# Half steps per head for layer 1's attention, gates ahead of branch products in `at`, and split folds

## The reference, cut to what matters

```python
for l in range(DEPTH):
    sh1, sc1, gt1, sh2, sc2, gt2 = adaln(c, w_ada[l], b_ada[l])     # silu(c) @ w_ada: [1024] x [1024, 6144]
    hx = modulate(rms_norm(x, g_mix[l]), sh1, sc1)
    px = split_cols(hx @ w_in[l], IN_SIZES)     # q, k, v, conv, short conv, fourier, 4 gates
    y_attn = windowed_latent_attention(q, k, v, kc, vc, sink)
    x = x + gt1 * mixer_output(px, y_attn, ...)
    x = x + gt2 * conv_ffn(modulate(rms_norm(x, g_ffn[l]), sh2, sc2), ...)

def mixer_output(p, y_attn, ...):
    y_conf, y_sc, y_fn = local_branches(...)    # y_conf = silu(layer_norm(dwconv31(a * sigmoid(g))))
    gates = split(sigmoid(p_gate), 4)
    m = gates[0] * (y_attn @ w_br[0])
    for g, y, w in zip(gates[1:], (y_conf, y_sc, y_fn), w_br[1:]):
        m = m + g * (y @ w)
    return m @ w_out
```

## Time and profile before

| | us |
|---|---|
| median of 3 runs | 1331.49 |
| lowest, highest | 1329.52, 1332.81 |
| the profiled execution's own time | 1331.0 |
| its span on the core | 1329.2 |
| around the span | 1.8 |

### The profile page before, as it was taken

One profiled execution on the slowest core, in us unless ns is written; L12 is line 12 of the kernel. 1 busy time (PEld: TensorE's weight loads), 2 busy tenths in 40 slices (PEclk: granted clock), 3 DMA queues, 4 the chain that ended last, 5 costly groups with the idle time before them and its releaser, 6 DMA issues.

```text
span 1329.2 us, 19887 instructions
## 1 busy us (share of the span) xinstructions
PE 1268.8 (95%) x7661; PEld 1096.8 (83%) x7661; DVE 884.4 (67%) x1203; ACT 555.7 (42%) x872; POOL 290.9 (22%) x247
## 2 busy tenths in 40 slices
PE   5999999999999999999999999999999998999997
PEld 3788877777788788787788888889878898999997
DVE  4694488653699568995756664576676566765654
ACT  4322345643343244331233332244566455653543
POOL 0003499111223001111001120003772130120210
PEclk9999999999999999999999999999999999999999
DMA  9463222213456315664555664235333454564560
GB/s 377 154 210 115 77 75 65 68 64 94 137 178 235 104 46 178 204 206 160 188 165 189 189 213 146 94 106 173 119 110 110 145 175 143 177 216 146 188 207 33
DMA packets 50339, 198.76 MB, mean 150 GB/s; under 512 B 5584, under 2 KB 6992, under 8 KB 49104
## 3 DMA queue, kind: packets, MB, share of 16 engines
q1 hardware_dynamic: 50256, 197.62, 45.3%
HBM read 196.55 MB, written 1.05 MB: 149 GB/s over the span
## 4 chain that ended last, share of the span: by engine, by line
PE 74%; DVE 17%; issue 5%; ACT 4%; DMA 0%; DVEq 0%; SPq 0%; ACTq 0%
PE psA L490 21%; PE psA L491 21%; PE psA L492 21%; DVE ada_sum L1228 4%; DVE w_lo L1207 4%; DVE acc L1443 2%; PE psB L490 2%; PE psB L492 2%; PE psB L491 2%; ACT w_hi L914 1%; DVE small L1456 1%; PE psB L759 1%; PE psB L747 1%; PE psB L663 1%; PE psA L732 1%
## 5 line engine op out<-in xcount | busy, mean ns | idle before, releaser
L490 PE MATMUL psA<-h_hi,w_hi 128*128 128x256 f32 (+1 forms) x1544 | 525.5, 340 | 9.0 <-DVE h_lo L1321 4.9
L491 PE MATMUL psA<-h_lo,w_hi 128*128 128x256 f32 (+1 forms) x1544 | 517.9, 335 | 0.0
L492 PE MATMUL psA<-h_hi,w_lo 128*128 128x256 f32 (+1 forms) x1544 | 517.8, 335 | 0.0
L914 ACT ACTIVATE w_hi<-raw 128x1024 fp32r<-128x1024 f32 (+2 forms) x244 | 277.0, 1138 | 341.5 <-PE psA L492 233.9
L1207 DVE TENSOR_TENSOR w_lo<-raw,w_hi 128x1024 fp32r<-128x1024 f32 (+2 forms) x244 | 332.8, 1364 | 127.8 <-ACT w_hi L914 127.1
L490 PEld LDWEIGHTS psA<-h_hi,w_hi 128*128 128x128 f32 x1544 | 296.4, 192 | 42.5 <-issue 7.6
L492 PEld LDWEIGHTS psA<-h_hi,w_lo 128*128 128x128 f32 x1544 | 296.3, 192 | 29.1
L491 PEld LDWEIGHTS psA<-h_lo,w_hi 128*128 128x128 f32 x1544 | 296.7, 192 | 28.1 <-issue 0.5
L479 POOL TENSOR_TENSOR hid_lo<-sig,hid_hi 128x512 f32 (+3 forms) x44 | 68.4, 1555 | 484.2 <-ACT hid_hi L1171 484.2
L1228 DVE SCALAR_TENSOR_TENSOR ada_sum<-raw,csil,ada_sum 128x1024 f32<-128x1024 f32 x112 | 158.2, 1443 | 0.0
L490 PE MATMUL psA<-hid_hi,w_hi 128*128 128x256 f32 (+1 forms) x352 | 118.4, 336 | 3.7 <-DVE sig L1634 2.1
(11 more groups left out here) (189 smaller groups left out, 1440.5 us busy)
## 6 DMA issues: line engine op xcount, KB each, us to landing
raw<-w_up SPq DMA_DIRECT2D x88, 512.0 KB, 4.2
raw<-w_ada SPq DMA_DIRECT2D x80, 512.0 KB, 3.5
raw<-w_dn SPq DMA_DIRECT2D x32, 704.0 KB, 5.0
raw<-w_in SPq DMA_DIRECT2D x36, 512.0 KB, 3.8
raw<-w_at SPq DMA_DIRECT2D x24, 512.0 KB, 3.5
raw<-w_fn SPq DMA_DIRECT2D x16, 640.0 KB, 3.9
raw<-w_sc SPq DMA_DIRECT2D x16, 640.0 KB, 3.9
raw<-w_cf SPq DMA_DIRECT2D x16, 640.0 KB, 4.0
```

Source lines behind the costliest of these rows:

```text
L490: pe.matmul(out, w0, hi, start=first, stop=False)
L491: pe.matmul(out, w0, lo, start=False, stop=False)
L492: return pe.matmul(out, w1, hi, start=False, stop=last)
L914: act.activation(w_hi[:, s, 0:tiles * P], raw[:, r, 0:tiles * P], ACT.Copy).then_inc(head_done, 1)
```

## The change

- In layer 1 a unit's two heads are weighed, turned and copied in two places rather than one: head 0 at place 2k (exp) and 2k+2 (turn), head 1 at 2k+1 and 2k+3; `values` comes at 2k+4. `share` stands at the start of ScalarE's place 2k+2, `weight_sum` behind the multiplication of the odd place.
- Layer 1 has two branch banks (`mix_bank`: psB[1], psB[3]) and turns both heads through psB[0]. Gates wait for the tanh two steps before, no longer for the multiplication.
- `at` follows the order `AT_ORDER`: (group, part), part 2 being the branch product. Gates stand one to two steps ahead of the branch products that they belong to; the layer norm's reciprocal moves from step 8 to 7, its silu from 9 to 8, its last rest from 10 to 9.
- The modulation groups 3 and 4 begin two steps later; the second of the two folds of a group moves one step on, and so does `REDUCE` for groups 3 to 7.
- SyncE's reload of `x` waits for the end of `at` as well, since `q` now holds gates.

```diff
-ADA_START = {2: START["in"] + 2, 3: START["at"] + 3, 4: START["at"] + 11}
+ADA_START = {2: START["in"] + 2, 3: START["at"] + 5, 4: START["at"] + 13}
...
-REDUCE = {START["out"] + 3 if _g == 4 else ADA_START[_g] + 10: _g for _g in ADA_START}
+REDUCE = {START["out"] + 4 if _g == 4 else ADA_START[_g] + 10 + (3 <= _g < 8): _g for _g in ADA_START}
+ADA_END = {ADA_START[_g] + 8: _g for _g in ADA_START}
+AT_ORDER = [(0, 0), (0, 1), (1, 0), (1, 1), (0, 2), (2, 0), (2, 1), (1, 2), (3, 0), (3, 1), (2, 2), (3, 2)]
...
+        def mix_bank(layer, n):
+            return psB[1] if layer and n % 2 else psB[3]
+        def turn_bank(layer, half):
+            return psB[0 if layer else half]
...
+        def halves_at(layer, place, late):
+            if layer == 0:
+                return [(place - late, half) for half in range(2)] if 0 <= place - late < NB[0] else []
+            k, half = divmod(place - late, 2)
+            return [(k, half)] if 0 <= k < NB[1] else []
+        LATE = [{"turn": 1, "value": 2}, {"turn": 2, "value": 4}]
...
                 for idx in range(LEN["sc"]):
-                    pe.wait_ge(evac, st.n - 1)
-                    merge(st, y_hi[:, 2:4, :], y_lo[:, 2:4, :], 2, 8 + idx, mix_bank,
-                          [(sc_rest, 2 * layer + 2), (evac, st.n)])
+                    pe.wait_ge(sigd, 34 * layer + 2 + 8 + idx - 1)
+                    merge(st, y_hi[:, 2:4, :], y_lo[:, 2:4, :], 2, 8 + idx, mix_bank(layer, st.n),
+                          [(sc_rest, 2 * layer + 2), (evac, st.n - layer)])
...
+                def turn(k, half):
+                    pe.wait_ge(pn, 2 * (b0 + k) + half + 1)
+                    if layer:
+                        pe.wait_ge(pt, 2 * (b0 + k) + half)
...
                         else:
-                            pe.wait_ge(evac, m0 + 3 * (group - 1))
+                            pe.wait_ge(sigd, 34 * layer + 18 + 2 * (group - 2) + part + 1)
...
                 def attend(place):
+                    k = at_place(layer, place, LATE[layer]["value"])
+                    if k is not None:
+                        attended(k)
+                    for k, half in halves_at(layer, place, LATE[layer]["turn"]):
+                        turned(k, half)
+                    for k, half in halves_at(layer, place, 0):
+                        weigh(k, half)
                 def attend_late(place):
+                    k = at_place(layer, place, LATE[layer]["turn"])
+                    if k is not None:
                         share(k)
...
+            def ada_fold(g, vv):
+                op = dve.tensor_reduce(ada_part[:, vv, :], ada_sum[:, vv, :].rearrange("p (b k) -> p b k", k=32),
+                                       AX.X, ALU.add, apply_transpose=True)
+                if vv == ada_vectors(8 * g) - 1:
                     op.then_inc(folded, 1)
...
+                    if st.n in ADA_END and ada_vectors(8 * ADA_END[st.n]) == 2:
+                        ada_fold(ADA_END[st.n], 1)
...
                         dve.scalar_tensor_tensor(t, sg, 1.0, ps, ALU.add, ALU.mult).then_inc(evac, 1)
+                        if place is not None and layer and place % 2:
+                            weight_sum(place // 2)
```

More of the change, by code:

```diff
@@ L326, in program, with at_place @@
         B0 = [0, NB[0]]
-        def step_at(layer, place):
-            k = place if layer == 0 else (place + 1) // 2 if place % 2 == 0 or place == 17 else None
-            return k
+        def at_place(layer, place, late):
+            count, every = NB[layer], 1 + layer
+            k, odd = divmod(place - late, every)
+            return k if odd == 0 and 0 <= k < count else None
+        def halves_at(layer, place, late):
[4 more added lines that the diff above has]
+        LATE = [{"turn": 1, "value": 2}, {"turn": 2, "value": 4}]
+        PLACES = [18, 19]
         def wide(layer, k):
@@ L462, in _ @@
                     add(n0 + START["sc"], idx, idx, gtmp[idx % 2])
-                for idx in range(2, LEN["at"], 3):
+                for group in range(4):
                     for half in range(2):
-                        add(n0 + START["at"], idx, idx // 3 * 2 + half, (gtmp if idx == 2 else tmp)[half])
+                        add(n0 + START["at"], 3 * group + 2, 2 * group + half, (gtmp if group == 0 else tmp)[half])
                 for idx in range(LEN["cf"]):
@@ L804, in _ @@
                     st = Step(m0 + idx, idx)
-                    group, part = divmod(idx, 3)
+                    group, part = AT_ORDER[idx]
                     pe.wait_ge(rest_done, st.n + 1)
@@ L1566, in _ @@
                                               ALU.subtract).then_inc(ln_rest, 1)
+                    if part == 2:
+                        for half in range(2):
+                            o = 2 * group + half
+                            if half == 0:
+                                dve.wait_ge(sigd, 34 * layer + 2 + 16 + o + 2)
+                                if group == 1:
+                                    dve.wait_ge(o_mm, b0 + len(un))
+                                dve.wait_ge(chunk_done, st.n + 1)
+                                dve.wait_ge(m_sum, 24 * layer + 8 + o)
+                            sg, t = (gsig, qsig, sig, qsig)[group][half], (gtmp if group == 0 else tmp)[half]
+                            op = dve.scalar_tensor_tensor(t[:, 0:T], sg[:, 0:T], 1.0,
+                                                          psB[2 * (group % 2) + half][:, 0:T], ALU.add, ALU.mult)
+                        op.then_inc(evac, 3)
+                    if idx == 4:
+                        dve.wait_ge(ln_mean, layer + 1)
+                        for c in range(2):
+                            dve.scalar_tensor_tensor(acc[:, c, 0:T], psB[2][:, 0:T], -float(D // CONF_W),
+                                                     acc[:, c, 0:T], ALU.mult, ALU.add).then_inc(ln_xc, 1)
+                    if layer == 0:
+                        if idx == 5:
+                            dve.wait_ge(m_sum, 10)
+                        ada_behind(st)
                 for idx in range(LEN["cf"]):
@@ L1757 @@
             arrays[f"w_{name}{layer}"] = chunks(np.concatenate([gates[b], br[b]], axis=1))
-        at_chunks = []
-        for o in range(0, KD, 2):
-            at_chunks += [gates[0][o], gates[0][o + 1], np.concatenate([br[0][o], br[0][o + 1]])]
+        at_chunks = [gates[0][2 * g + part] if part < 2 else np.concatenate([br[0][2 * g], br[0][2 * g + 1]])
+                     for g, part in AT_ORDER]
         arrays[f"w_at{layer}"] = chunks(np.stack(at_chunks))
```

185 lines of the change are left out of this document (71 added, 114 removed).

## The result

| | before | after |
|---|---|---|
| median, 9 runs each | 1330.8 | 1324.33 |
| lowest, highest | 1328.91, 1332.82 | 1320.71, 1326.48 |
| the profiled execution | 1331.0 | 1320.71 |

The ratio after to before is 0.9948, 95% interval 0.9935 to 0.9962: 6.9 us less (5.1 to 8.6). The forecast was 1320, range 1311.5 to 1326.5. The profiled execution of the changed kernel is the shortest of its nine, 3.6 us under their median, where that of before lay at its median. So the profiles show 10.3 us of gain and the medians 6.5; the last part of the account comes back to that.

What follows compares the result with a forecast made beforehand. TensorE, busy for 1268.8 us, was taken as the bound, so only its idle time could be won. The terms 4.0 + 0.8 + 0 + 3.0 + 2.8 = 10.6 came off 1331.0, giving 1320.4, stated as 1320, range 1311.5 to 1326.5.

Steps and rivals of the forecast that it cites:

- `at` in layer 0: Layer 0's `at`: gates ahead of the branch products cover two unnamed TensorE waits; gain 4.0 us, bounds 2.7 and 4.0.
- `out`: Layer 0's `out`: the 1.62 us wait for `w_lo` goes, half given back to the later reduction; gain 0.8, bounds 0 and 1.6.
- `up0`: VectorE is full there, so the 2.0 us fold wait passes to `dn0`'s first product; gain 0, bounds -1.3 and +1.0.
- `dn0`: The 1.7 us fold wait goes, with the 1.3 us of slow clock behind it; gain 3.0, bounds 1.7 and 3.0.
- Layer 1: Bank waits go but the `share` chain lengthens to 11.7 us per pair; with `at`, gain 2.8, bounds -2.1 and 10.6.
- The shared port: VectorE contends with GpSimd for SBUF; left out of the sum, by the rule it adds 3.5 us in layer 1, giving 1324.
- B: Rival, chance 0.18: TensorE bounds layer 1, the chain being shorter than counted; layer 1 gives 10.6 and the time is 1312.6.
- C: Rival, chance 0.18: longer chain per pair, or clock falls at the turn; 3.5 to 6 us more, about 1325, up to 1327.
- A: The forecast itself, chance 0.52: 1320, with its own range of 1316 to 1324.
- D: Rival, chance 0.08: the waits only move, layer 1 grows by 2 and layer 0's terms come back; 1328 to 1331.
- E: Rival, chance 0.04: slower, TensorE's clock staying at the 1.2 GHz level over layer 1's branch steps; 1336 and more.

Runs made afterwards that it cites:

- split_not5: The changed kernel with only group 5, whose reduction stands in `up0`, folded together again and reduced at its old step: median 1321.30, ratio 0.9923 to the kernel before.
- head_first: The changed kernel with `w_hi` ahead of `share` on ScalarE in layer 1's even places: median 1315.52, ratio 0.9883 to the kernel before.
- folds_back: The changed kernel with both folds of each group together again and reductions at their old steps: median 1327.29, ratio 0.9963 to the kernel before.
- at_alone: The changed kernel cut to the new `at` order and moved layer norm: whole units, one branch bank, folds together; median 1327.42, ratio 0.9959 to the kernel before.
- before_head_first: The kernel before with one swap alone, `w_hi` ahead of `share` in layer 1's branch steps: median 1326.77, ratio 0.9964 to the kernel before.
- three_both_layers: three_edits with `w_hi` ahead of `share` in layer 0 as well: median 1310.84, ratio 0.9845 to the kernel before.
- three_edits: The changed kernel with layer 1's `w_hi` ahead of `share`, group 5 folded and reduced as before, group 4's reduction one step later: median 1312.11, ratio 0.9864.

## Why the prediction came out, point by point

- **`at` in layer 0, 4.0.** Right: 5.1 by the trace. Both unnamed waits are gone, and a wait of 0.3 us for a reduction with them; 0.8 us is unassigned.
- **`out`, 0.8.** The 1.62 us wait went, as said. The half that was to be given back was 0.97 us at the reduction; by the start of `up0` the stage had lost 0.2 us in all. The other 0.9 us came at the norm, where the clock was low twice as long; that stretch differs between other kernels whose `out` is the same, so I don't put it down to the change.
- **`up0`, 0, with a bound of -1.3.** This is the step that failed. The wait of 2.0 us did pass on to the first product of `dn0`, which grew to 4.05 and not 3.5. But behind it the clock was low for two windows, and this took 2.7 us. The bound had the right mechanism at half its size, and the wrong chance. split_not5 shows it from the other side. The 2.7 us are those of this kernel's two profiles: in head_first the same wait of 4.05 us has one window at 0.50 behind it, and the two stages take 165.2 us and not 166.4.
- **`dn0`, 3.0.** Right: the wait of 1.7 us and the slow window near 643 are gone. folds_back against split_not5 gives 3.6 us for it, and at_alone, where no low clock follows that wait of 1.73, 1.8. With the line above, the two stages gave 0.2 instead of 3.0.
- **Layer 1, 2.8.** The mechanism was right: the bank waits went, the same time returned as waits for exp and `share`, and the chain runs through the added `w_hi`, which head_first shows. The size was off: 4.9 us. The period did it: it was 11.2 in the mean and not 11.7, being 12.4 only beside GpSimd's taps, 10.9 behind them and 10.4 and 9.4 with the smaller chunks at the end, which the forecast did not count. Over seven pairs that is 3.4 us. The first `share` took 1.5 back: it came at 941.0 in a trace that runs 6.5 us ahead at the start of layer 1, so at 947.5 on the scale on which the forecast had 946.0. So the branch steps lost nothing (0.3 gained), and `at` gave its waits and slow window back whole, 1.0 + 2.3 + 1.3 = 4.6. Of these the 1.3 belong to the execution as much as to the program: before_head_first has both waits without the slow window.
- **The shared port.** The forecast took `w_lo` as it stood, 1.48. It rose to 2.03 in contended pairs, more than the 0.25 per start of the estimate by the rule. What the Trainium skill says there of holding the pair for a whole instruction it says of VectorE's 2-port modes, and the forecast took it for two-input instructions too; the two pairs of `ada_sum` and `hid_lo` above agree with that, since each time the second one took 1.0 to 1.1 us more. The time by the rule, 1324, is the measured median, but not for that reason: in the profile, where the port's cost shows, the time is 1320.7.
- **The rivals.** B did not happen, but its size was real: with the chain cut, layer 1's stage gives 12.0 us (head_first), where B had 10.6. C did in part, in the pairs of 12.4 and 12.5 us, but not in the mean; the median, 1324.3, still lies nearer its 1325 than A's 1320, for reasons that are open (below). D did not happen, and neither did E; the clock stayed at 1.00 in layer 1's branch steps.
- **The sum.** Worked against the profile, 1320.4 was forecast and 1320.7 came. That is partly luck: 1.6 us of lead came from the start-up, which no term held, and +2.1 in layer 1 (with the new wait in front of `fn` already taken off), +1.1 in `at`, -1.0 in `out`, -2.8 in `up0` and `dn0` and -1.1 at a norm (low clock for two windows rather than one) nearly cancel. Against the medians the forecast of 10.6 us less was too much: 6.5 came.

**What stays open** is why most timed runs of the changed kernel take some 4 us more than its profiled ones. The profiles of the other kernels, whose first 1350 matmuls are in the same order as in this one, show where that much can lie. Matmul 600 starts at 132.0 to 133.2 in some and at 135.1 to 135.5 in others; and by matmul 1350 a further 2 us is lost in some, in waits for exp and `share` near 203 us. 1320.7 + 2.5 + 2 = 1325.2 would be such an execution of the changed kernel, and its highest run is 1326.5. That its slower runs are these was not seen, since both its profiled executions took the shorter course. Between matmul 2400 and 3150, too, executions can lie 4 us apart, as three_both_layers shows, and whether that happens to the changed kernel is open as well.

## What to carry to other kernels

Idle time of a second engine in front of an instruction is room for whatever stands behind it in that engine's queue: look there before restructuring the work, since moving one copy ahead of one scaling was worth more than half steps and two banks. A bank that is waited for is often only the place where a chain between two other engines shows; a second bank moves the wait to the next thing that the chain makes. Two shorter waits can be cheaper than the one into which they are gathered, so where an engine behind TensorE is full, count not only the wait that goes but the one into which it is gathered, and what the clock does behind it.

## What the runs showed of the hardware

- Waits of 2.01 and 1.30 us, 67 us apart, left the granted clock at 1.00 (split_not5, three_edits); waits of 3.04 and 2.81 at the same places were followed by one window of 3.4 us at 0.50 (three_both_layers). One of 4.05 at the second place was followed by two in the changed kernel, 14 matmuls of 512 columns where full speed would have given 26, and by one in head_first.
- The length of a wait alone did not decide it. The same wait of 1.73 us in `dn0` was followed by a window at 0.50 in folds_back and by none in at_alone; the one of 2.31 us in layer 1's `at` by one in the kernel before and by none in before_head_first; and for the one of 2.73 us in layer 0's `at` it was the other way round.
- Beside GpSimd's two-instruction taps a `w_lo` of 128 x 1280 took up to 2.03 us and a tap of 128 x 256 up to 0.98; alone 1.49 and 0.48. With `ada_sum` and GpSimd's `hid_lo`, the one that started first kept its length (1.28 and 1.48 us) and the other took 1.0 to 1.1 us more.
- Kernels whose program is the same up to there start matmul 600 at 132.0 to 133.2 us in some profiles and at 135.1 to 135.5 in others.
